# Prompt attention in a one-layer decoder step: mask and maximum in one operation, absorption in four parts, key products and output halves moved to other slots

## The reference

```
def mla_prompt(q_nope, q_rope, rows, lp):
    c, kr = rows[..., :KV_LORA_RANK], rows[..., KV_LORA_RANK:]
    k_nope = jnp.einsum('bsc,chd->bshd', c, lp["w_uk"])
    v = jnp.einsum('bsc,chd->bshd', c, lp["w_uv"])
    ...                                   # for each block of 128 queries:
        s = (einsum('bqhd,bkhd->bhqk', qn_b, k_nope) + einsum('bqhr,bkr->bhqk', qr_b, kr)) * MLA_SCALE
        s = jnp.where(kpos[None, :] <= qpos[:, None], s, -jnp.inf)
        p = jax.nn.softmax(s, axis=-1).astype(v.dtype)
        return jnp.einsum('bhqk,bkhd->bqhd', p, v)

def mla_sample(q_nope, q_rope, new_rows, cache_l, page_table, lp):
    q_lat = jnp.einsum('bthd,chd->bthc', q_nope, lp["w_uk"])      # "absorption"
    ...
    s_new = einsum('bthc,bkc->bhtk', q_lat, nc) + einsum('bthr,bkr->bhtk', q_rope, nr)
```

## Time and profile before

| | us |
|---|---|
| median of 3 runs | 1081.08 (1078.83 to 1081.27) |
| the profiled execution | 1080.94 |
| its span in the trace | 1078.7 |
| PE busy | 1010.3 (94%) |
| PEld busy | 903.9 (84%) |
| DVE busy | 517.9 (48%) |
| ACT busy | 303.7 (28%) |
| POOL busy | 454.1 (42%) |

### The profile page before, as it was taken

How to read it: one execution, slowest core, us unless ns; L and a number is a source line. 1 busy time by engine, 2 the same in 40 slices (tenths; PEclk the granted TensorE clock), 3 DMA queues, 4 the chain that set the end, 5 groups by cost and what they waited for, 6 DMA issues and landing times.

```text
span 1078.7 us, 19052 instructions
## 1 busy us (share of the span) xinstructions
PE 1010.3 (94%) x8116; PEld 903.9 (84%) x8116; DVE 517.9 (48%) x723; ACT 303.7 (28%) x619; POOL 454.1 (42%) x297
## 2 busy tenths in 40 slices
PE   2899978978899999899999999999999999999997
PEld 2889967855666666599996579999999999999997
DVE  2788968358655555446225436541143124214413
ACT  3523245436444444212014412220021002001222
POOL 1554466530011111255522026555565656555561
PEclk9899989989999999999999999999999999999998
DMA  6323234540436666452239012232323233232322
GB/s 175 106 59 79 78 113 143 127 149 1 176 117 264 266 263 254 139 195 79 88 122 386 11 38 81 79 98 79 98 80 96 81 86 91 84 94 80 97 78 83
DMA packets 144009, 129.78 MB, mean 120 GB/s; under 512 B 13093, under 2 KB 136882, under 8 KB 140086
## 3 DMA queue, kind: packets, MB, share of 16 engines
q1 hardware_dynamic: 138550, 88.10, 27.1%
q0 software_dynamic: 2304, 37.75, 9.1%
q10 hardware_dynamic: 3072, 2.72, 0.8%
HBM read 123.53 MB, written 5.03 MB: 119 GB/s over the span
## 4 chain that ended last, share of the span: by engine, by line
PE 79%; DVE 9%; ACT 3%; issue 2%; DMA 2%; POOL 2%; SPq 2%; ACTq 0%; DVEq 0%; POOLq 0%
PE gps L557 55%; PE gps L861 6%; PE aux L877 3%; PE aux L897 2%; PE gps L988 1%; PE gps L1063 1%; POOL wlo L487 1%; PE aux L872 1%; PE aux L812 1%; DMA wraw<-in_w_q_up_dram 1%; PE gps L834 1%; PE aux L1001 1%; DMA wraw<-in_w_mem_v_dram 1%; PE aux L1022 1%; PE aux L887 1%
## 5 line engine op out<-in xcount | busy, mean ns | idle before, releaser
L557 PE MATMUL gps<-act_hi,whi 128*128 128x272 f32 x944 | 275.5, 292 | 8.8 <-DVE act_lo L1545 6.4
L474 POOL TENSOR_SCALAR whi<-wraw 128x1024 fp32r<-128x1024 f32 (+1 forms) x110 | 114.1, 1038 | 385.2 <-PE gps L557 276.9
L557 PE MATMUL gps<-act_lo,whi 128*128 128x272 f32 x944 | 274.5, 291 | 0.0
L557 PE MATMUL gps<-act_hi,wlo 128*128 128x272 f32 x944 | 273.9, 290 | 0.0
L477 POOL TENSOR_TENSOR wlo<-wraw,whi 128x1024 fp32r<-128x1024 f32 (+1 forms) x110 | 260.1, 2365 | 9.2
L557 PEld LDWEIGHTS gps<-act_hi,whi 128*128 128x128 f32 x944 | 179.4, 190 | 9.6 <-issue 6.4
L557 PE MATMUL gps<-h_hi,whi 128*128 128x272 f32 x640 | 185.7, 290 | 0.0
L557 PE MATMUL gps<-h_lo,whi 128*128 128x272 f32 x640 | 185.1, 289 | 0.0
L557 PE MATMUL gps<-h_hi,wlo 128*128 128x272 f32 x640 | 184.6, 288 | 0.0
L557 PEld LDWEIGHTS gps<-act_hi,wlo 128*128 128x128 f32 x944 | 179.4, 190 | 0.0
L557 PEld LDWEIGHTS gps<-act_lo,whi 128*128 128x128 f32 x944 | 179.2, 190 | 0.0
(11 more groups left out here) (356 smaller groups left out, 1496.8 us busy)
## 6 DMA issues: line engine op xcount, KB each, us to landing
wraw<-in_w_up_dram SPq DMA_DIRECT2D x32, 512.0 KB, 4.1
wraw<-in_w_down_dram SPq DMA_DIRECT2D x32, 512.0 KB, 3.9
wraw<-in_w_in_dram SPq DMA_DIRECT2D x14, 512.0 KB, 4.0
kv<-in_cache_mem_k_dram SPq DMA_DIRECT2D x7, 1024.0 KB, 7.8
kv<-in_cache_mem_v_dram SPq DMA_DIRECT2D x7, 1024.0 KB, 12.5
wraw<-in_w_mem_k_dram SPq DMA_DIRECT2D x8, 512.0 KB, 3.9
wraw<-in_w_mem_v_dram SPq DMA_DIRECT2D x8, 512.0 KB, 3.9
wraw<-in_w_out_dram SPq DMA_DIRECT2D x8, 512.0 KB, 4.3
```

Source lines behind the costliest of these rows:

```text
L474: nc.gpsimd.tensor_scalar(whi[:, slot, 0:n], wraw[:, slot, 0:n], 1.0, 1.0, ALU.mult, ALU.mult).then_inc(pool_step, 1)
L557: mm = nc.tensor.matmul(out_of(a), w_of(w, k), x_of(x, k, part), start=(k == 0 and s == 0), stop=(k == k_tiles - 1 and s == 2))
```

## The change

The mask becomes a tile `wide` of 512 columns, zero but for the last 128, which are the causal mask. It lies where the rows' stores have their source, so VectorE waits for these stores and fills it ahead of the loop. One VectorE operation then adds its last w columns to the scores, writes the negated sum back and accumulates its minimum, which is the negated maximum; the exponential has scale -1. The key product of the next pair moves from slots 0, 8, 16 to 3, 11, 19, and its two halves are copied one each in slots 4 and 5 of the pair, behind the transposed copy. Weight turns move to slots 21 to 24 and their copies to 22 to 25, the absorption is issued two heads at a time in slots 26 to 29, the new rows in slot 32, and what follows them is moved along. VectorE writes the low half of outputs one slot later.

```diff
@@ -193,6 +193,7 @@
         pb = [at(f"pb{i}", [128, 512], F32, o) for i, o in enumerate((M0 + 16384, M0 + 18432, COS0, COS0 + 2048))]
         pT = at("pT", [128, 2, 4, 512], F32, M0 + 20480)
         sm = at("sm", [128, 3, 32], F32, M0 + 36864)
+        wide = at("wide", [128, 512], F32, R0)
 
         cT = at("cT", [128, 2, 2048], F32, M0 + 18432)
         ropT = at("ropT", [128, 512], F32, M0 + 34816)
@@ -766,15 +767,17 @@
                     mm = nc.tensor.transpose(W_BANK[0:64, 128 * i:128 * i + 128], wraw[:, U_UK % 2, o:o + 64], ident[:, :])
                 mm.then_inc(wk_T, 1)
 
-            def absorb():
-
-                pe.wait_ge(wk_ev, 4)
-                for h in range(H):
+            def absorb(g):
+
+                if g == 0:
+                    pe.wait_ge(wk_ev, 4)
+                for h in (2 * g, 2 * g + 1):
                     for c in range(2):
                         mm = nc.tensor.matmul(W_BANK[:, (c * H + h) * TS:(c * H + h + 1) * TS],
                                               wukT[:, h, 128 * c:128 * c + 128], q[0:64, h, TP:T],
                                               start=True, stop=True)
-                mm.then_inc(ql_ps, 1)
+                if g == 3:
+                    mm.then_inc(ql_ps, 1)
 
             def new_rows():
 
@@ -803,7 +806,7 @@
             for n in range(4 * H + 5):
                 if n < 4 * H:
                     h, i = 2 * (n // 8) + n % 2, n % 8 // 2
-                    if n % 8 == 0 and n // 8 + 1 < 4:
+                    if n % 8 == 3 and n // 8 + 1 < 4:
                         k_pair(n // 8 + 1)
                     if n % 8 == 0:
                         pe.wait_ge(k_ok, n // 8 + 1)
@@ -835,11 +838,11 @@
                                                   vn[:, kt, 64 * h:64 * h + 64], pT[:, e, kt, 128 * i:128 * i + 128],
                                                   start=(kt == 0), stop=(kt == i), skip_group_check=True)
                     mm.then_inc(at_pv, 1)
-                if 18 <= n <= 24 and n % 2 == 0:
-                    absorb_turn((n - 18) // 2)
-                if n == 27:
-                    absorb()
-                if n == 30:
+                if 21 <= n <= 24:
+                    absorb_turn(n - 21)
+                if 26 <= n <= 29:
+                    absorb(n - 26)
+                if n == 32:
                     new_rows()
 
             def turn(n):
@@ -1347,30 +1350,30 @@
                 act.sem_inc(v_ok, 1)
 
 
-            def k_copy(j):
+            def k_copy(j, e):
 
                 t = T_UK + j
-                act.wait_ge(tile_done, t + 1)
-                if j >= 2:
-                    act.wait_ge(at_s, 8 * (j - 1))
-                step(nc.scalar.copy(Kb[0:64, (2 * j) % 4, :], gps[0:64, 2 * (t % 2), :]))
-                step(nc.scalar.copy(Kb[0:64, (2 * j + 1) % 4, :], gps[64:128, 2 * (t % 2), :]))
-                act.sem_inc(tile_free[t % 2], 1)
-                act.sem_inc(k_ok, 1)
+                if e == 0:
+                    act.wait_ge(tile_done, t + 1)
+                    if j >= 2:
+                        act.wait_ge(at_s, 8 * (j - 1))
+                step(nc.scalar.copy(Kb[0:64, (2 * j + e) % 4, :], gps[64 * e:64 * e + 64, 2 * (t % 2), :]))
+                if e:
+                    act.sem_inc(tile_free[t % 2], 1)
+                    act.sem_inc(k_ok, 1)
 
             T_BANK = (gps[:, 1, :], aux[:, 3, :])
             act.wait_ge(k_rope, 4)
-            k_copy(0)
+            k_copy(0, 0)
+            k_copy(0, 1)
             for n in range(4 * H + 6):
                 if n < 4 * H:
-                    if n % 8 == 0 and n // 8 + 1 < 4:
-                        k_copy(n // 8 + 1)
                     w = 128 * (n % 8 // 2 + 1)
                     act.wait_ge(at_nm, n + 1)
                     if n >= 4:
                         act.wait_ge(at_T, n - 3)
                     nc.scalar.activation(pb[n % 4][:, 0:w], aux[:, n % 3, 0:w], ACT.Exp, bias=sm[:, 0, n:n + 1],
-                                         scale=1.0, accum_out=sm[:, 1, n:n + 1]).then_inc(at_exp, 1)
+                                         scale=-1.0, accum_out=sm[:, 1, n:n + 1]).then_inc(at_exp, 1)
                 m = n - 3
                 if 0 <= m < 4 * H:
                     j, i = m // 8, m % 8 // 2
@@ -1380,17 +1383,19 @@
                     nc.scalar.copy(pT[:, m % 2, 0:i + 1, 128 * i:128 * i + 128],
                                    T_BANK[m % 2][:, 0:128 * (i + 1)].rearrange("p (k n) -> p k n", n=128)
                                    ).then_inc(at_pT, 1)
+                if n < 24 and n % 8 in (4, 5):
+                    k_copy(n // 8 + 1, n % 8 - 4)
                 m = n - 6
                 if m >= 0 and m % 8 == 7:
                     j = m // 8
                     act.wait_ge(at_pv, 4 * j + 4)
                     nc.scalar.copy(act_hi[:, j, 0:TP], gps[:, 3 - 3 * (j % 2), :]).then_inc(at_hi, 1)
-                if 19 <= n <= 25 and n % 2:
-                    g = (n - 19) // 2
+                if 22 <= n <= 25:
+                    g = n - 22
                     act.wait_ge(wk_T, g + 1)
                     nc.scalar.copy(wukT[:, 2 * g:2 * g + 2, :],
                                    gps[0:64, 2, :].rearrange("p (h n) -> p h n", h=2)).then_inc(wk_ev, 1)
-                if n == 33:
+                if n == 35:
                     act.wait_ge(new_dve, 1)
                     for g in range(2):
                         nc.scalar.activation(pn[:, g, :], gps[:, 2, 32 * g:32 * g + 32], ACT.Exp, bias=nmn[:, g:g + 1],
@@ -1781,7 +1786,7 @@
                                        q[R, :, TP:T].rearrange("p h (b t) -> p h b t", t=TD)))
                 elif n == 24:
                     step(V.tensor_reduce(pick[:, :], ident[:, :].rearrange("p (j q) -> p q j", j=4), AX, ALU.add))
-                elif n == 28:
+                elif n == 30:
                     dve.wait_ge(ql_ps, 1)
                     for c in range(2):
                         ins = V.tensor_copy(qlat[:, c, :, :].rearrange("p b (h t) -> p h b t", t=TD),
@@ -1789,18 +1794,22 @@
                         if c == 0:
                             step(ins)
                     ins.then_inc(ql_ok, 1)
-                elif n == 32:
+                elif n == 34:
                     dve.wait_ge(new_pe, 1)
                     step(V.tensor_reduce(sn[:, 0, :], gps[:, 2, 0:64].rearrange("p (g k) -> p g k", g=2), AX, ALU.max))
                     V.tensor_scalar(nmn[:, :], sn[:, 0, :], -1.0, None, ALU.mult).then_inc(new_dve, 1)
 
-            for n in range(4 * H + 6):
+            dve.wait_ge(row_out[0], 32)
+            dve.wait_ge(row_out[1], 32)
+            step(V.memset(wide[:, 0:384], 0.0))
+            step(V.tensor_copy(wide[:, 384:512], causal[:, :]))
+            for n in range(4 * H + 7):
                 if n < 4 * H:
                     w = 128 * (n % 8 // 2 + 1)
                     dve.wait_ge(at_s, n + 1)
-                    dg = aux[:, n % 3, w - 128:w]
-                    step(V.tensor_tensor(dg, dg, causal[:, :], ALU.add))
-                    V.tensor_reduce(sm[:, 0, n:n + 1], aux[:, n % 3, 0:w], AX, ALU.max, negate=True).then_inc(at_nm, 1)
+                    s = aux[:, n % 3, 0:w]
+                    V.tensor_tensor_reduce(s, s, wide[:, 512 - w:512], -1.0, 3.0e38, ALU.add, ALU.min,
+                                           sm[:, 0, n:n + 1]).then_inc(at_nm, 1)
                 m = n - 1
                 if 0 <= m < 4 * H:
                     w = 128 * (m % 8 // 2 + 1)
@@ -1808,9 +1817,9 @@
                     step(V.reciprocal(sm[:, 1, m:m + 1], sm[:, 1, m:m + 1]))
                     V.tensor_scalar(pb[m % 4][:, 0:w], pb[m % 4][:, 0:w], sm[:, 1, m:m + 1], None, ALU.mult
                                     ).then_inc(at_p, 1)
-                if 18 <= n <= 32:
+                if 18 <= n <= 34:
                     absorbed(n)
-                m = n - 6
+                m = n - 7
                 if m >= 0 and m % 8 == 7:
                     j = m // 8
                     dve.wait_ge(at_hi, j + 1)
```

## The result

| | before | after |
|---|---|---|
| median, us | 1080.70 (1078.46 to 1083.98, 20 runs) | 1086.40 (1084.24 to 1096.83, 20 runs) |
| the profiled execution, us | 1080.94 | 1087.46 |
| its span, us | 1078.7 | 1085.2 |
| ratio, 95% interval | | 1.0078 [1.0056, 1.0099] |

The account below looks back on a forecast made before the run. TensorE was taken to bound the kernel, so prompt attention's gains or losses pass one for one to the end. Terms -1.7 +0.3 -1.9 +5.4 -4.5 +1.2 make -1.2 us, from 1080.94 to 1079.7 us; 8-in-10 range 1075.0 to 1084.5.

Parts of the forecast that it names:

- Mask and maximum in one operation: Prompt attention, score products of slots 0 to 8: 0.23 us saved per item on the path, -1.7 us in all.
- Key products inside a pair: Score products of slots 8 to 16: +0.3 us, with slot 14 waiting for the key copy; slots 16 to 21: -1.9 us.
- Weight turns: Slots 21 to 24: each turn waits for a copy in its own slot, nothing overlaps; 14.5 us for 9.06, +5.4.
- Absorption and the clock: Slots 25 to 31: new rows leave and the clock stays up, -4.5 us; new rows lengthen the tail, +1.2.
- Second halves a slot later: Low halves of outputs: VectorE no longer waits for ScalarE's high half, but this gives nothing.
- The clock falls in the serial slots: Slots 21 to 24 and those behind: low clock adds 5.7 us, giving 1085.4 us; chance 0.10.
- The weight turns find their copies in time: Slots 21 to 24 overlap like their neighbours, so the 5.4 us isn't paid: 1074.3 us; chance 0.19.
- The slow fused operation: VectorE's fused mask and maximum runs below one element a cycle: +6.2 us, 1085.9 us; chance 0.06.

Follow-up runs that it names:

- e1: Kernel before with the fused mask and maximum alone; 1077.84 us, ratio 0.9970 to before.
- e7: e2 with the key products of pairs 1 and 2 in slots 3 and 11, copies at the end of slots 4, 5, 12, 13; 1079.16 us, 0.9983 to before.
- e2: Changed kernel with weight turns, their copies and key products back in their old slots; 1077.71 us, ratio 0.9951 to before.
- e4: Changed kernel with weight copies and key copies at the head of their ScalarE slots, ahead of the exponential; 1077.19 us, ratio 0.9960 to before.
- e5: Kernel before with the absorption in four parts (slots 26 to 29) and the new rows in slot 32; 1081.58 us, ratio 1.0004 to before.
- e11: e4 with the new rows in slot 31 instead of 32; 1076.53 us, ratio 0.9965 to before.
- e12: Changed kernel with the new rows in slot 31 instead of 32; 1089.62 us, ratio 1.0063 to before.
- e13: Changed kernel with mask add and maximum as two operations again, no wide mask; 1092.77 us, ratio 1.0110 to before.
- e14: Kernel before with VectorE's low halves of outputs a slot later, nothing else; 1080.50 us, ratio 0.9992 to before.
- e6: Kernel before with weight turns in slots 21 to 24 and their copies in slots 22 to 25, nothing else; 1091.28 us, ratio 1.0097 to before.
- e15: e6 with the four weight copies at the head of ScalarE's slots 22 to 25; 1079.59 us, ratio 0.9984 to before.
- e3: Changed kernel with the weight copies at the head of ScalarE's slots 22 to 25, ahead of the exponential; 1081.99 us, ratio 1.0007 to before.
- e10: e8 with key products of pairs 1 and 2 in slots 3 and 11, key copies at the head of slots 4, 5, 12, 13; 1075.91 us, 0.9958 to before.
- e9: e2 with the absorption in one piece again, so before plus fused operation and later low halves; 1076.53 us, ratio 0.9955 to before.
- e16: Second run of e9, the same kernel; 1076.86 us, ratio 0.9953 to before.
- e8: e2 with the new rows in slot 31 instead of 32; 1074.97 us, ratio 0.9958 to before.

## Why the prediction was wrong

By its own steps, in the order of the sum.

*Mask and maximum in one operation: right in the link, wrong in its use.* Fused operation to exponential at 512 is 300.82 to 301.60, 0.78, where it was 1.06: 0.28 saved, I took 0.23. The accumulator's read is hidden: the next reciprocal starts while it runs. But eight links in S0 to S8 gave 0.9 (e1), not 1.8: slots 4, 5 and 6 became 0.27, 0.32 and 0.28 shorter, the others not at all, so VectorE bounded three slots and not eight. Another 1.4 came from the key product (S0 to S8 is 7.49 in e7, 8.93 in e2), which I had counted as one lost and one gained; in slot 3 it costs nothing, and at slot 8's head it had cost its whole length. 7.48 for 8.1 is two errors that cancel in part, and so luck.

*Key products inside a pair: the chain right, one wait left out.* I forecast +0.3 for S8 to S16, it was +1.45. e4 takes it back to 11.88, so the copies' place costs 1.9 there: 1.24 in slot 14 (2.78 for e4's 1.54), the wait that I named and counted at 1.0, and 0.67 in slot 8 (2.30 for e4's 1.63), which I hadn't. There the transposed copy stands behind the key copy of slot 5 (247.95) and an exponential, and TensorE waits 0.78 for it (249.96).

*Weight turns: right, mis-sized by 1.8.* Slot 22 took 4.04, forecast 4.04. Slot 21 took 4.46 for 3.57: its exponential began 2.36 after S21, 0.7 later than I had. It stood behind the first key copy, slot 20's, on ScalarE (272.20, then 272.96 for `Kb`), a link that I left out; and its fused operation began only at 272.21, 1.61 after S21, behind a copy of qropez on VectorE (271.89) that I had put at nothing. Key copy and fused operation both end at 272.78, so neither alone is shown to be the cause. Slots 23 and 24 took 4.57 and 3.20 for 4.14 and 2.74, at the low clock: 0.9 together.

*Absorption and the clock: the step that failed.* "Cut into four with full products between them I expect it to stay." The term was -4.5 +1.2, together -3.3; in the changed kernel the two segments together took 22.57 for 22.63, so -0.1. In S25 to S31 of this execution it did (11.88 for 11.3), but then it fell in the tail: from 303.8 to the page turn at 309.44 TensorE had no wait and half the clock, so the same work would have taken 2.8 less, and the tail 7.9, as forecast (8.1). e5 shows the term alone: I had -4.5 and +1.2, it measured -3.7 and +3.7, of which the 3.5 us at the low clock are 1.8. Nor do parts keep the clock up in S25 to S31: in the profiled executions of e7, e11, e12 and e13, which all have them, part of that stretch ran at 0.50. So the forecast's reason, that a block of 32-column products makes the clock fall, isn't borne out: it fell with the block cut up too, and in e14 at 284.2, in the middle of the block (281.9 to 287.1). VectorE also came late in the tail: the copies of qlat (0.88) and the low half (0.68) stood ahead of slot 31's fused operation, which began 2.07 after S31 (before: 1.17); the new rows covered it.

*Second halves a slot later: forecast at nothing.* The medians say the same (e14), but the segments don't: S16 to S25 became 1.6 shorter. In that execution the gain was given back at the low clock behind it. In e6, which lacks this edit, slot 22's mask add began 2.0 later after its score product than the 1.17 of the earlier trace rows, behind the low half.

So the 7.8 between the forecast and the profiled execution (1087.46, which is 1.1 above the median) are: ahead of the stage 1.7, S0 to S21 0.7, slot 21 0.9, the clock in slots 23 and 24 0.9, S25 to S31 0.6, tail 2.6 (the clock), and 0.4 of rounding and page loop.

*The rivals.* "The clock falls in the serial slots" had the right sign and by chance the right time (1085.4), with a chance of 0.10, too little. I held against it that TensorE kept its clock with single waits over 1 us; four such slots in a row were another thing. Its price was wrong: in these slots 0.9 instead of 4.3, and the rest by a second fall that it didn't have. "The weight turns find their copies in time" was wrong as to the copies' place, but it is what e15 and e4 do: 1074.3 forecast, 1077.2 measured. The slow fused operation fell (0.698 at 512, it needed 0.95).

*What stays open.* Why the clock falls behind the weight turns, and when. In the profiled executions it fell in the tail of after, e2, e3, e4, e5 and e10, between S25 and S31 in before, e1, e6, e9, e14, e15 and e16, between S25 and S31 and on into the tail in e7, e11, e12 and e13, and not at all behind S25 in e8; the low stretches there lasted from 3.4 to 24 us. Executions of one kernel differ too: of after, those with a mean granted clock of 0.980 took 1084.2 to 1086.1, those with 0.969 to 0.973 took 1090 to 1097. By an estimate from these numbers, 0.010 of the mean clock over 1090 us is 22 us more at half clock, up to 11 us of time, so the clock can account for the long executions, and it takes more of it than the one fall in the tail (6.9 us). Where in the kernel it lay in them is not recorded. No experiment here set the fall or took it away for good, so that the clock is why this step failed is read from the traces and not shown by an edit.

## What to carry to other kernels

Where an engine's slot holds the exponential of this slot and a copy that another engine waits for in the same slot, put the copy first: its input is ready, the exponential's isn't. Ask for each moved step what stands ahead of it on its engine's queue, and whether that is younger work; here the order inside a slot was worth 9 to 13 us, the number of turns nothing. And price the granted clock with every serial stretch: it makes a loss larger than the sum of its waits (e6: 10.5 measured, 4 to 5 expected from the waits), and a gain in one stretch may be given back where the clock falls instead (e5, e14). No version here is clearly better than the kernel before with the fused operation and the low halves a slot later (e9, e16, 0.4 to 0.5% faster); e8 and e10 are equal to it.

## What the runs showed of the hardware

- VectorE's operation with an accumulated output took 301, 432, 564 and 698 ns at 128, 256, 384 and 512 columns (after; one input in PSUM and one in SBUF, float32), where the plain maximum before took 291, 424, 557 and 691: no more than 10 ns for the second input and the accumulation. The separate read of the accumulator took 136 ns and overlaps the next operation.
- The granted clock fell to 0.50 after a stretch in which TensorE was busy for about half (4.47 of 9.30 us, 270.6 to 279.9), and also after one in which it was busy for 16.59 of 16.80 us (287.0 to 303.8). In profiled executions of kernels with the same code up to S0, that score product starts up to 3.3 us apart.
